# A staggered RWKV stage: the order of the chunks inside a step is reversed, and its stores are issued by ScalarE instead of GpSimd

## The chip, the cores and the metric

One Trainium2 chip, one of its cores. The metric is the device time of the whole program in microseconds (us), lower is better; a run gives one time, and the median of several is compared.

## The reference, cut to what matters

The program computes one inference step of two decoder layers. The change lies in layer 0 alone: the RWKV-7 scan over 2048 prompt tokens (8 heads of 64), and the S5 state-space layer (32 groups of 16 channels, 64 complex states each) that runs beside it.

```python
def rwkv7_scan(r, decay, k, v, aa, bb, s0):
    def step(s, inp):
        r_t, w_t, k_t, v_t, a_t, b_t = inp
        sa = jnp.einsum('bhvk,bhk->bhv', s, a_t)
        s = s * w_t[:, :, None, :] + sa[..., None] * b_t[:, :, None, :] + v_t[..., None] * k_t[:, :, None, :]
        return s, jnp.einsum('bhvk,bhk->bhv', s, r_t)
...
# s5_mixer: h = associative scan of abar * h + B u, per group
y = jnp.einsum('btgp,gcp->btgc', h_re, c_re) - jnp.einsum('btgp,gcp->btgc', h_im, c_im)
y = jax.nn.gelu(y.reshape(bsz, t, D_B) + d_skip * u)
```

## The kernel before, in words

The program is a row of stages with a barrier between any two: projections, the stage of this study (`rwkv_chunks`, names `rc_...`), the samples, an output stage, and the second layer. Everything is float32. In every stage each engine has its own list of instructions, and semaphores order them; an engine executes its list strictly in order.

`rwkv_chunks` cuts the 2048 tokens into 32 chunks of 64. One chunk goes through 16 phases, and in nearly all of them TensorE makes small 64x64 products (eight tiles, four of them side by side in the array), after which either ScalarE copies the PSUM banks to SBUF or VectorE masks or adds them, and the next phase of the same chunk needs that result:

- phase 0 (`M_`): products of the operands (L1652, L1655); VectorE masks them (L1800, L1802, L1806).
- phase 1 (`KV`): L1664, L1668; ScalarE copies all of it (L1766, 1,024 elements a partition). In phase 2 GpSimd masks a part in place (L1842).
- phases 2 to 11: five levels of a triangular inverse. The even ones (U0 to U4; L1729 to L1741) end in a copy by ScalarE (L1782), the odd ones (X0 to X4; L1750, for X4 L1752) in a predicated copy by VectorE (L1826).
- phase 12 (`SOLVE`, L1675, copied by ScalarE L1770), phase 13 (`LINK`, L1683, VectorE L1809 and L1812), phase 14 (`STATE`, L1695 to L1701, VectorE L1821), phase 15 (`OUT`, L1708 to L1714, ScalarE L1776 into `yb`).

The chunks are staggered: chunk c is in phase t - 6c at step t (`LAG` is 6, `FLIGHT` is 3), 202 steps in all. So six steps make one chunk's worth of work, and in each of these six there are two or three chunks on the way, six phases apart: {0, 6, 12}, {1, 7, 13}, {2, 8, 14}, {3, 9, 15}, {4, 10}, {5, 11}. `running(t)` gives them in the order in which every engine writes them into its list: in the kernel before the newest chunk (lowest phase) first.

A chunk's result `yb` goes to memory by two DMAs (even chunks) or four (odd chunks), issued by GpSimd at the end of its part of phase 15 (L1848, L1852). `yb` has two buffers; ScalarE waits for the store of the chunk two before.

The S5 layer rides along: after the chunks' phases of a step, each engine appends its S5 part. VectorE makes tables (L1383, L1435, L1439 and others) in every step up to 103 and again between the two halves. In steps 52 to 68 TensorE transposes two groups of a table (L1343 to L1345), ScalarE copies them (L1296) and GpSimd stores them (L1323); the next transposes wait for that copy (`tb_ev`). In steps 103 to 139 and 165 to 201 one group is treated every two steps: TensorE L1353 at odd steps and L1367 to L1369 at even ones, VectorE rotations and a scan, GELU on ScalarE at odd steps (L1303), and a store by GpSimd (L1328). The next group's L1367 to L1369 wait for that GELU (`y_ev`).

Of the kernel before, what the change touches and what calls it, by code (L numbers as in the profile page):

```python
# [25 lines left out]
SEQ = 2048  # L26
# [4 lines left out]
NCH = SEQ // CH  # L31
# [183 lines left out]
class Tail:  # L215
# [229 lines left out]
    def gpsimd(self, pool):  # L445
        def weights(k):
            pool.wait_ge(self.w_high, k + 1)
            low_part(pool, self.wl[:, k], self.wr[:, k % 4], self.wh[:, k]).then_inc(self.w_low[0], 1)

        def low(t):  # L450
            h, n = t % 2, self.rows(t)
            c = slice(h * P, h * P + n) if t < TT else slice(0, n)
            pool.wait_ge(self.c_high, t + 1)
            low_part(pool, self.cl[h][:, :, 0:n], self.cb[t // 2 % 2][:, :, c], self.ch[h][:, :, 0:n]).then_inc(self.c_low, 1)
        weights(0)
        weights(2)
        low(0)
        weights(4)
        weights(6)
        for t in range(1, TT + 1):  # L460
            low(t)
# [705 lines left out]
G, SP_, GC = 32, 64, 16  # L1167
T8 = 8
NC8 = SEQ // T8
HG = G // 2  # L1170
# [4 lines left out]
class StateSpace:  # L1175
# [102 lines left out]
    def scalar(self, act, t):  # L1278
        c_ = lambda n: self.sc[:, n, :]
        if t == self.BEGIN:  # L1280
            act.wait_ge(self.cst, 16 * self.MAPS)
            act.activation(c_(0), self.pt[:, 2, :], ACT.Exp).then_inc(self.act0, 1)
        if t == self.BEGIN + 2:
            act.wait_ge(self.angles, 1)
            act.activation(c_(1), c_(14), ACT.Exp)
            act.activation(c_(20), c_(14), ACT.Exp, scale=float(T8)).then_inc(self.act0, 1)
        if t == self.BEGIN + 4:
            act.wait_ge(self.angles, 2)
            act.activation(c_(5), c_(4), ACT.Sin)
            act.activation(c_(6), c_(4), ACT.Sin, scale=0.5).then_inc(self.act0, 1)  # L1290
        i = t - self.LT - 1
        if 0 <= i < HG:
            act.wait_ge(self.tb_pe, i + 1)
            if i >= 2:
                act.wait_ge(self.bi_st[i % 2], 16 * (i // 2))
            act.copy(self.bi[i % 2][:, :, :].rearrange("p a c -> p (a c)"), self.bx[:, :]).then_inc(self.tb_ev, 1)  # L1296
        g = self.group(t - 3)
        if g is not None:
            q = g % 2
            act.wait_ge(self.y_pe, g + 1)  # L1300
            if g >= 2:
                act.wait_ge(self.y_st[q], 16 * (g // 2))
            act.activation(self.yo[q][:, :], self.by[:, 0:NC8], ACT.Gelu_apprx_tanh).then_inc(self.y_ev, 1)  # L1303

    def scalar_end(self, act):
        for q in (0, 1):
            act.wait_ge(self.y_st[q], 16 * HG)
# [3 lines left out]
    def gpsimd(self, pool, t):  # L1311
        g = self.group(t + 1)
        if g is not None:
            k, at = g // 8, g % 8 * GC
            pool.wait_ge(self.tq_in[k % 2], 16 * T8 * (k // 2 + 1))
            if g >= 2:
                pool.wait_ge(self.y_pe, g - 1)
            pool.tensor_copy(self.tp[g % 2][:, :].rearrange("p (t c) -> p t c", t=T8),
                             self.tq[k % 2][:, :, at:at + GC]).then_inc(self.tp_ok, 1)
        i = t - self.LT - 1  # L1320
        if 0 <= i < HG:
            pool.wait_ge(self.tb_ev, i + 1)
            pool.dma_start(self.trans[:, i], self.bi[i % 2][:, :, :]).then_inc(self.bi_st[i % 2], 16)  # L1323
        g = self.group(t - 3)
        if g is not None:
            at = g % 8 * GC
            pool.wait_ge(self.y_ev, g + 1)
            pool.dma_start(self.y[at:at + GC, g // 8, 0:SEQ].rearrange("c (t n) -> t c n", t=T8), self.yo[g % 2][:, :]  # L1328
                           ).then_inc(self.y_st[g % 2], 16)

# [214 lines left out]
PHASES = 6 + 2 * LEVELS  # L1547
(M_, KV, U0) = range(3)
FLIGHT, LAG = 3, 6
SOLVE, LINK, STATE, OUT_ = range(PHASES - 4, PHASES)  # L1550
# [3 lines left out]
def rwkv_chunks(nc, ops, wc, const, y, s_out, space):  # L1554
# [7 lines left out]
    with Stage(nc, "rc") as s_:  # L1562
# [10 lines left out]
        yb = [s_.sb(f"yb{q}", [P, 4, CH]) for q in (0, 1)]  # L1573
# [16 lines left out]
        y_st = [s_.sem("y_st0"), s_.sem("y_st1")]  # L1590
        block = s_.block()
        half = [slice(0, 64), slice(64, 128)]
        quads = ((0, 0), (1, 1), (0, 1), (1, 0))
        tiles = [(g, r, s) for g in (0, 1) for r, s in quads]
        STEPS = LAG * (NCH - 1) + PHASES
        running = lambda t: [(c, t - LAG * c) for c in range(NCH - 1, -1, -1) if 0 <= t - LAG * c < PHASES]
        tokens = lambda c: slice(c * CH, (c + 1) * CH)
        every = lambda ap, n: ap.rearrange("p (o c) -> p o c", o=1).broadcast_to([P, n, ap.shape[-1]])
        flat = lambda ap: ap.rearrange("p s g c -> p s (g c)")
# [160 lines left out]
        @block.scalar  # L1760
        def _(act):
            def phase(c, ph):
                q, b = c % FLIGHT, bk[c % FLIGHT]
                if ph == KV:
                    act.wait_ge(k_pe, c + 1)
                    act.copy(kt[q][:, :, :, :].rearrange("p s k c -> p (s k c)"), b[:, :, :].rearrange("p s c -> p (s c)")  # L1766
                             ).then_inc(k_sb, 1)
                elif ph == SOLVE:
                    act.wait_ge(gh_pe, c + 1)
                    act.copy(hg[q][:, :, :, :, :].rearrange("p s g n c -> p s (g n c)"), b[:, :, 0:4 * CH]  # L1770
                             ).then_inc(gh_sb, 1)
                elif ph == OUT_:
                    act.wait_ge(y_pe, c + 1)
                    if c >= 2:
                        act.wait_ge(y_st[c % 2], STORES[c % 2] * (c // 2))
                    act.copy(yb[c % 2][:, :, :].rearrange("p (s k) c -> p s (k c)", s=2), b[:, :, 2 * CH:4 * CH]  # L1776
                             ).then_inc(y_sb, 1)
                elif U0 <= ph < SOLVE and ph % 2 == 0:
                    n = (ph - U0) // 2
                    act.wait_ge(u_pe[n], c + 1)  # L1780
                    lo, count = ((LV_u, 4), (LV_W, 3), (LV_u, 2))[min(n, 2)]
                    act.copy(lv[q][:, :, lo:lo + count].rearrange("p s k g c -> p s (k g c)"), b[:, :, 0:count * 2 * CH]  # L1782
                             ).then_inc(u_sb[n], 1)
            for t in range(STEPS):
                for c, ph in running(t):
                    phase(c, ph)
                s5.scalar(act, t)
            s5.scalar_end(act)
            for q in (0, 1):
                act.wait_ge(y_st[q], STORES[q] * NCH // 2)  # L1790
# [43 lines left out]
        @block.gpsimd  # L1834
        def _(pool):
            pool.wait_ge(cst, 64)

            def phase(c, ph):
                if ph == U0:
                    pool.wait_ge(k_sb, c + 1)  # L1840
                    k = kt[c % FLIGHT][:, :, 0:4].rearrange("p s k c -> p s (k c)")
                    pool.tensor_tensor(k, k, every(mask[:, :], 2), ALU.mult).then_inc(k_ok, 1)  # L1842
                elif ph == OUT_:
                    pool.wait_ge(y_sb, c + 1)
                    out = y[:, :, tokens(c)]
                    if c % 2 == 0:
                        for s in (0, 1):
                            pool.dma_start(out[:, s::2], yb[0][:, 2 * s:2 * s + 2, :]).then_inc(y_st[0], 16)  # L1848
                    else:
                        for r in (0, 1):  # L1850
                            for h in (0, 1):
                                pool.dma_start(out[half[h], r::2], yb[1][half[r], 2 * h:2 * h + 2, :]  # L1852
                                               ).then_inc(y_st[1], 16)
            for t in range(STEPS):
                for c, ph in running(t):
                    phase(c, ph)
                s5.gpsimd(pool, t)
# [1147 lines left out]
def program(nc, I, O):  # L3005

    def scratch(name, shape):
# [11 lines left out]
    space = (u, I["s5_par"], I["s5_mats"], I["s5_skip"], I, y_b, O["s5_p"], (kept_l, kept_m, kept_a),  # L3019
             scratch("s5_trans", (P, G // 2, 2, 2 * P)), scratch("s5_lags", (15 * GC, G * GC)))  # L3020
    rwkv_chunks(nc, ops, wc, I, y_a, O["rwkv_p"], space)
    even_samples(nc, vecs, I["state_rwkv"], O["rwkv_s"], y_a, u_s, I["s5_in"], kept_l, kept_m, kept_a, I["s5_drow"], I, y_b,
                 O["s5_s"])
# [129 lines left out]
```

## Time and profile before

| | us |
|---|---|
| median of 3 runs | 3392.26 |
| lowest, highest | 3385.58, 3393.54 |
| the profiled execution, its own time | 3385.58 |
| its span, first to last instruction | 3383.8 |
| the stage `rwkv_chunks` in it | 672 to about 1256 |
| TensorE, VectorE, ScalarE, GpSimd busy in the whole span | 2894.4, 2180.0, 1232.0, 823.6 |

The span is 1.8 us shorter than the time of the same execution. Times in the rows are microseconds from the span's start. PE is TensorE's matmul, PEld its weight load, DVE is VectorE, ACT ScalarE, POOL GpSimd, SP SyncE; a q behind an engine marks its sequencer, where DMAs are issued. One matmul in the source stands in the trace as two records or passes, since the operands are float32. Where a row says "issue", the engine waited for nothing that the profile shows.

### The profile page before, as it was taken

Reading aid. Unit: us, or ns where it says so; the run is one execution under the profiler, and the core shown is the slowest. Engines: PE = TensorE matmul, PEld = TensorE weight load, DVE = VectorE, ACT = ScalarE, POOL = GpSimd, SP = SyncE. Lnnn points to the kernel's source line nnn. Section 1 sums busy time; section 2 is a strip of 40 time slices with the busy share of each in tenths; the row PEclk is TensorE's granted clock in tenths of the full one; section 3 lists DMA queues with packets and bytes.
Section 4 is the critical chain, followed back from the end, with each engine's and each line's share of the span. In section 5 each row is a group of like instructions: output and inputs, shape, how many; then the busy total and the mean of one; then the engine's idle time right before and its main releaser. Section 6 shows DMA issues by size and latency. Waiting matters only on the chain. (4 is left out here: it accounts for less than half of the span.)

```text
span 3383.8 us, 77001 instructions
## 1 busy us (share of the span) xinstructions
PE 2894.4 (86%) x31187; PEld 2423.5 (72%) x31187; DVE 2180.0 (64%) x3314; ACT 1232.0 (36%) x2205; POOL 823.6 (24%) x726
## 2 busy tenths in 40 slices
PE   8799999867788772899789999997878898987698
PEld 7699999866677651688589878775755666667476
DVE  3435566567677655777618777723437898886587
ACT  1015555433333322344111110101107888884432
POOL 4100000012222220211112111103115676664221
PEclk9899999989999995999889999998998999999899
DMA  4425545443434335464448999964541101006542
GB/s 162 166 79 147 158 145 153 139 98 94 110 98 114 92 110 161 140 175 137 148 147 253 360 329 356 333 220 154 178 128 62 64 1 64 14 14 187 193 149 89
DMA packets 468650, 500.76 MB, mean 148 GB/s; under 512 B 199169, under 2 KB 362226, under 8 KB 463290
## 3 DMA queue, kind: packets, MB, share of 16 engines
q1 hardware_dynamic: 371162, 332.45, 32.9%
q10 hardware_dynamic: 88176, 146.58, 12.5%
q0 software_dynamic: 8960, 16.81, 1.8%
q8 instruction: 248, 4.06, 0.5%
q14 instruction: 104, 0.85, 0.1%
HBM read 357.52 MB, written 138.41 MB: 147 GB/s over the span
## 5 line engine op out<-in xcount | busy, mean ns | idle before, releaser
L2487 POOL TENSOR_TENSOR sp_att<-sp_beta,sp_left 128x512 f32<-128x512 f32 (+3 forms) x320 | 317.9, 1003 | 195.7 <-DVE sp_left L2443 184.0
L102 PE MATMUL po_acc<-po_x_high,po_w_low 128*128 128x412 f32 (+1 forms) x840 | 306.0, 364 | 33.9 <-POOL po_w_low L95 15.0
L102 PE MATMUL pe_acc<-pe_x_high,pe_w_low 128*128 128x412 f32 (+1 forms) x840 | 304.8, 363 | 22.8 <-DVE pe_x_low L95 14.1
L103 PE MATMUL po_acc<-po_x_low,po_w_high 128*128 128x412 f32 (+1 forms) x840 | 298.6, 355 | 0.0
L104 PE MATMUL po_acc<-po_x_high,po_w_high 128*128 128x412 f32 (+1 forms) x840 | 298.1, 355 | 0.0
L104 PE MATMUL pe_acc<-pe_x_high,pe_w_high 128*128 128x412 f32 (+1 forms) x840 | 295.8, 352 | 0.0
L103 PE MATMUL pe_acc<-pe_x_low,pe_w_high 128*128 128x412 f32 (+1 forms) x840 | 295.8, 352 | 0.0
L2443 DVE TENSOR_TENSOR_SCAN sp_left<-sp_z,sp_left,sp_zero 128x512 f32<-128x512 f32 x192 | 235.3, 1266 | 14.1 <-ACT sp_z L2387 12.1
L2174 DVE TENSOR_TENSOR po_work<-po_work,po_q 128x1024 f32<-128x1024 f32 x128 | 173.2, 1353 | 83.6 <-DMA po_work<-in_cache_k 78.1
L102 PEld LDWEIGHTS po_acc<-po_x_high,po_w_low 128*128 128x128 f32 x840 | 161.9, 193 | 82.2 <-ACT po_o L801 33.2
L2379 ACT ACTIVATE sp_beta<-sp_z,sp_bias 128x512 f32<-128x512 f32 (+3 forms) x320 | 183.5, 631 | 72.1 <-PE sp_z L2318 44.2
L1842 POOL TENSOR_TENSOR rc_kt<-rc_kt,rc_mask 128x512 f32<-128x512 f32 x32 | 40.7, 1273 | 681.9 <-ACT rc_kt L1766 681.7
L801 ACT COPY po_o<-po_acc 128x412 f32<-128x412 f32 (+1 forms) x105 | 52.5, 500 | 391.9 <-PE po_acc L104 375.4
L1782 ACT COPY rc_lv<-rc_bk 128x512 f32<-128x512 f32 (+2 forms) x160 | 109.8, 715 | 217.7 <-PE rc_bk L1741 217.4
L102 PEld LDWEIGHTS pe_acc<-pe_x_high,pe_w_low 128*128 128x128 f32 x840 | 159.8, 190 | 36.7 <-issue 24.6
L2387 ACT ACTIVATE sp_z<-sp_z,sp_bias_neg 128x512 f32<-128x512 f32 (+3 forms) x320 | 179.7, 614 | 0.0
L2333 PE MATMUL sp_t<-sp_id,sp_att 128*128 128x128 f32 x1088 | 154.7, 280 | 24.2 <-ACT sp_aT L2393 18.9
L2333 PEld LDWEIGHTS sp_t<-sp_id,sp_att 128*128 128x128 f32 x1088 | 117.4, 142 | 67.8 <-issue 64.9
L2348 PE MATMUL sp_ob<-sp_aT,sp_v 128*64 128x128 f32 x2176 | 155.2, 281 | 9.1 <-DVE sp_g L2457 9.1
L103 PEld LDWEIGHTS po_acc<-po_x_low,po_w_high 128*128 128x128 f32 x840 | 162.1, 193 | 0.9
L104 PEld LDWEIGHTS po_acc<-po_x_high,po_w_high 128*128 128x128 f32 x840 | 161.8, 193 | 0.7
L103 PEld LDWEIGHTS pe_acc<-pe_x_low,pe_w_high 128*128 128x128 f32 x840 | 159.6, 190 | 1.6
(453 smaller groups left out, 7308.3 us busy)
## 6 DMA issues: line engine op xcount, KB each, us to landing
po_work<-in_cache_k SPq DMA_DIRECT2D x256, 256.0 KB, 4.9
po_work<-in_cache_v ACTq DMA_DIRECT2D x256, 256.0 KB, 4.5
scratch_ops<-pe_work SPq DMA_DIRECT2D x160, 128.0 KB, 2.0
out_z<-pe_o SPq DMA_DIRECT2D x84, 206.0 KB
out_z<-po_o ACTq DMA_DIRECT2D x84, 206.0 KB
pe_w<-in_w_e SPq DMA_DIRECT2D x21, 512.0 KB
po_w<-in_w_o ACTq DMA_DIRECT2D x21, 512.0 KB
rc_opx<-scratch_ops SPq DMA_DIRECT2D x16, 640.0 KB, 6.1
```

The lines of the kernel that those rows point to most:

```text
L102: pe.matmul(out, ll, rh, start=start, stop=False)
L103: pe.matmul(out, lh, rl, start=False, stop=False)
L104: return pe.matmul(out, lh, rh, start=False, stop=stop)
L801: copy(self.ot[:, t % self.PIECES, 0:hi - lo], bank[:, 0:hi - lo]).then_inc(self.evicted, 1)
L1782: act.copy(lv[q][:, :, lo:lo + count].rearrange("p s k g c -> p s (k g c)"), b[:, :, 0:count * 2 * CH]).then_inc(u_sb[n], 1)
L2174: dve.tensor_tensor(kp[:, p % KR], kp[:, p % KR], qb[:, b % 2:b % 2 + 1, :].broadcast_to([P, 2, CW]), ALU.mult).then_inc(prod, 1)
L2333: mm = pe.transpose(tb[h][:, b * P:(b + 1) * P], att[h][:, n % 3, b * P:(b + 1) * P], idt[:, :])
L2348: mm = pe.matmul(ob[tile(n) % 2][c, 0:P], vt[m % 2][:, 4 * g + b, c], aT[h][:, n % 2, b * P:(b + 1) * P], start=(diagonal(n) and b == 0), ...
L2379: act.activation(be[h][:, n % 4, 0:w], zb[h][n % 2][:, 0:w], ACT.Sigmoid, scale=DC ** -0.5, bias=bt[:, head:head + 1]).then_inc(sig[h], 1)
L2387: act.activation(zb[h][n % 2][:, 0:w], zb[h][n % 2][:, 0:w], ACT.Sigmoid, scale=-DC ** -0.5, bias=nbt[:, head:head + 1]).then_inc(kept[h], 1)
L2443: dve.tensor_tensor_scan(row[:, at:at + w][:, ::-1], zb[h][n % 2][:, 0:w][:, ::-1], zero.broadcast_to([P, w]), start, ALU.mult, ALU.add).t ...
L2487: pool.tensor_tensor(att[h][:, n % 3, 0:w], be[h][:, n % 4, 0:w], left[h][tile(n) % 2][:, at + 1:at + 1 + w], ALU.mult).then_inc(at_ok[h], 1)
```

## The change

Two things change, both in the stage `rwkv_chunks`.

1. `running(t)` lists the chunks of a step in ascending order: the oldest chunk (highest phase) comes first, the newest last. All four engines' lists are reordered alike. No instruction is added or taken away by this.
2. All stores of the stage are issued by ScalarE. Right behind the copy (or GELU) that fills the buffer it waits for its own semaphore and issues the DMAs: two or four per chunk (`yb`), one per S5 group (`yo`), one per step of the transposes (`bi`). GpSimd keeps the masking and the copies of `tq`.

```diff
@@ StateSpace.scalar
             act.copy(self.bi[i % 2][:, :, :].rearrange("p a c -> p (a c)"), self.bx[:, :]).then_inc(self.tb_ev, 1)
+            act.wait_ge(self.tb_ev, i + 1)
+            act.dma_start(self.trans[:, i], self.bi[i % 2][:, :, :]).then_inc(self.bi_st[i % 2], 16)
...
             act.activation(self.yo[q][:, :], self.by[:, 0:NC8], ACT.Gelu_apprx_tanh).then_inc(self.y_ev, 1)
+            act.wait_ge(self.y_ev, g + 1)
+            act.dma_start(self.y[at:at + GC, g // 8, 0:SEQ].rearrange("c (t n) -> t c n", t=T8), self.yo[q][:, :]
+                          ).then_inc(self.y_st[q], 16)
@@ StateSpace.gpsimd
-        i = t - self.LT - 1
-        if 0 <= i < HG:
-            pool.wait_ge(self.tb_ev, i + 1)
-            pool.dma_start(self.trans[:, i], self.bi[i % 2][:, :, :]).then_inc(self.bi_st[i % 2], 16)
...
-            pool.wait_ge(self.y_ev, g + 1)
-            pool.dma_start(self.y[at:at + GC, g // 8, 0:SEQ].rearrange("c (t n) -> t c n", t=T8), self.yo[g % 2][:, :]
-                           ).then_inc(self.y_st[g % 2], 16)
@@ rwkv_chunks
-        running = lambda t: [(c, t - LAG * c) for c in range(NCH - 1, -1, -1) if 0 <= t - LAG * c < PHASES]
+        running = lambda t: [(c, t - LAG * c) for c in range(NCH) if 0 <= t - LAG * c < PHASES]
@@ rwkv_chunks, scalar, phase OUT_ (and taken out of gpsimd, phase OUT_)
+                    act.wait_ge(y_sb, c + 1)
+                    out = y[:, :, tokens(c)]
+                    if c % 2 == 0:
+                        for s in (0, 1):
+                            act.dma_start(out[:, s::2], yb[0][:, 2 * s:2 * s + 2, :]).then_inc(y_st[0], 16)
+                    else:
+                        for r in (0, 1):
+                            for h in (0, 1):
+                                act.dma_start(out[half[h], r::2], yb[1][half[r], 2 * h:2 * h + 2, :]
+                                              ).then_inc(y_st[1], 16)
```

## Rows read from the trace of the kernel before

**Rows 1.** Page, part 1: busy time, share of the span, instructions.
```profile
PE 2894.4 (86%) x31187; PEld 2423.5 (72%) x31187; DVE 2180.0 (64%) x3314; ACT 1232.0 (36%) x2205; POOL 823.6 (24%) x726
```

**Rows 2.** Stage by stretches: start:end, length, busy (count), clock, DMA share, GB/s.
```profile
708.40:824.80 116.40, 81.27 (x3604) 73.56 (x3604) 88.95 (x171) 38.24 (x59) 22.37 (x28) 0.96 0.35 76
824.80:869.00 44.20, 33.86 (x1144) 31.65 (x1144) 25.53 (x56) 16.58 (x30) 12.94 (x20) 1.00 0.42 122
869.00:948.20 79.20, 57.64 (x2580) 51.48 (x2580) 58.09 (x158) 27.73 (x44) 17.97 (x24) 0.98 0.40 97
964.30:1073.20 108.90, 102.94 (x3232) 84.92 (x3232) 76.91 (x195) 38.13 (x66) 33.47 (x55) 1.00 0.49 119
1073.20:1158.30 85.10, 58.37 (x2569) 52.20 (x2570) 57.66 (x125) 26.87 (x42) 16.87 (x23) 0.96 0.34 77
```

**Rows 3.** Waits of PE, 676 to 1245 us: total us, times, longest.
```profile
PE rc_bk L1738 <- issue: 19.9, 16, 3.4
PE rc_bk L1664 <- DVE rc_m L1802: 17.7, 17, 5.6
PE rc_s_x L1343 <- ACT rc_s_bi L1296: 11.8, 12, 1.4
```

**Rows 4.** DMA queues, 676 to 1245 us: packets, MB, share of 16 engines.
```profile
q8 instruction: 132, 2.16, 1.6%
```

**Rows 5.** Stretches between two pauses of PE (columns as in rows 2).
```profile
721.09:726.10 5.01, 3.15 (x128) 2.79 (x131) 3.74 (x9) 1.66 (x3) 0.00 (x0) 1.00 0.06 16
...
762.15:766.03 3.88, 2.52 (x128) 2.17 (x127) 2.93 (x6) 1.50 (x2) 0.00 (x0) 1.00 0.17 35
```

**Rows 6.** Timeline of PE, one such stretch: start, us, instruction, [idle before <- releaser].
```profile
762.15 0.39 PE L1738 MATMUL rc_bk<-rc_xx,rc_m 64*64 64x64 f32 x10 [0.74 <-issue]
762.32 0.45 PE L1741 MATMUL rc_bk<-rc_id,rc_xx 64*64 64x64 f32 x16
762.55 0.45 PE L1738 MATMUL rc_bk<-rc_xx,rc_m 64*64 64x64 f32 x16
...
766.03 0.38 PE L1750 MATMUL rc_bk<-rc_lv 64*64 64x64 f32 x9 [1.34 <-issue]
```

**Rows 7.** Timelines of ACT, then PE, then DVE, over phases 5 and 0.
```profile
784.49 0.80 ACT L1782 COPY rc_lv<-rc_bk 128x768 f32<-128x768 f32 x1 [0.33 <-PE rc_bk L1741]
786.69 0.58 ACT L1782 COPY rc_lv<-rc_bk 128x512 f32<-128x512 f32 x1 [1.40 <-PE rc_bk L1741]
...
787.33 0.62 PE L1752 MATMUL rc_bk<-rc_lv 64*64 64x64 f32 x14 [0.45 <-ACT rc_lv L1782]
...
791.01 0.72 PE L1664 MATMUL rc_bk<-rc_opx 64*64 64x128 f32 x13 [1.42 <-DVE rc_m L1802]
...
788.06 0.45 DVE L1826 COPY_PREDICATED rc_lv<-rc_lev,rc_bk 128x256 f32<-128x256 int32 x1 [0.69 <-PE rc_bk L1752]
788.40 0.68 DVE L1383 TENSOR_TENSOR rc_s_tmp<-rc_s_m,rc_s_sc 128x512 f32<-128x512 f32 x1
...
789.84 0.42 DVE L1800 TENSOR_TENSOR rc_xx<-rc_bk,rc_lev 128x256 f32<-128x256 f32 x1
790.18 0.68 DVE L1802 TENSOR_TENSOR rc_m<-rc_bk,rc_mask 128x512 f32<-128x512 f32 x1
```

**Rows 8.** Timeline in the stretch of the transposes.
```profile
841.64 0.33 PE L1343 MATMUL rc_s_x<-rc_s_id,rc_s_cos 128*128 128x128 f32 x1 [1.43 <-ACT rc_s_bi L1296]
...
843.18 0.59 ACT L1296 COPY rc_s_bi<-rc_s_x 128x512 f32<-128x512 f32 x1 [1.59 <-DMA scratch_s_trans<-rc_s_bi]
```

**Rows 9.** DMA issues: one on ACT's timeline; a line of SP, ns min/median/max.
```profile
41.50 0.33 ACTq L210 DMA_DIRECT2D scratch_u<-pu_o  x1
...
L1614 SPq DMA_DIRECT2D rc_opx<-scratch_ops x64: 586/646/1508, 680.9 to 1195.0; - x64
```

**Rows 10.** Groups of the whole span: busy us, mean ns | idle before.
```profile
L1303 ACT ACTIVATE rc_s_yo<-rc_s_y 128x256 f32<-128x256 f32 x32 | 12.4, 387 | 9.6 <-PE rc_s_y L1369 9.6
...
L1353 PE MATMUL rc_s_x<-rc_s_xT,rc_s_bi 128*128 128x256 f32 x128 | 36.2, 405 | 0.0
```

More of the change, by code:

```diff
@@ L1296, in scalar @@
             act.copy(self.bi[i % 2][:, :, :].rearrange("p a c -> p (a c)"), self.bx[:, :]).then_inc(self.tb_ev, 1)
+            act.wait_ge(self.tb_ev, i + 1)
+            act.dma_start(self.trans[:, i], self.bi[i % 2][:, :, :]).then_inc(self.bi_st[i % 2], 16)
         g = self.group(t - 3)
         if g is not None:
-            q = g % 2
+            q, at = g % 2, g % 8 * GC
             act.wait_ge(self.y_pe, g + 1)
@@ L1319, in gpsimd @@
                              self.tq[k % 2][:, :, at:at + GC]).then_inc(self.tp_ok, 1)
-        i = t - self.LT - 1
-        if 0 <= i < HG:
-            pool.wait_ge(self.tb_ev, i + 1)
-            pool.dma_start(self.trans[:, i], self.bi[i % 2][:, :, :]).then_inc(self.bi_st[i % 2], 16)
-        g = self.group(t - 3)
-        if g is not None:
-            at = g % 8 * GC
-            pool.wait_ge(self.y_ev, g + 1)
-            pool.dma_start(self.y[at:at + GC, g // 8, 0:SEQ].rearrange("c (t n) -> t c n", t=T8), self.yo[g % 2][:, :]
-                           ).then_inc(self.y_st[g % 2], 16)
     def tensor(self, pe, t):
@@ L1842, in phase @@
                     pool.tensor_tensor(k, k, every(mask[:, :], 2), ALU.mult).then_inc(k_ok, 1)
[L1843 to L1853, printed above, removed]
             for t in range(STEPS):
```

## The prediction

> **What bounds the kernel now.** I read the page first, then the stage by stretches, then PE's waits in it, the DMA queues, and timelines. TensorE is busy 86% of the span [rows 1], and the change touches one stage of some 580 us. There the stretches differ [rows 2]. In two of them, where S5 groups run, PE is at its work: from 964 to 1073 it is busy 102.94 of 108.90, and from 1158 to 1245 it is alike. The rest is different: in 708 to 825 PE is busy 81.27 of 116.40, though ACT is busy only 38.24 and DVE 88.95. So there something paces PE that is not an engine's work.
>
> The waits say what. The largest is "issue" [rows 3], and on the timeline such pauses cut PE's list in regular pieces: one at 762.15, the next at 766.03, in the middle of a row of equal matmuls, with 128 matmuls and 127 or 128 weight loads between them [rows 5, 6]. The instruction queue moved 132 transfers of 2.16 MB in 569 us [rows 4]: 16 KB each, which is 64 bytes for each of 256 instructions. So PE eats one such block and waits for the next. A block that ends in a pause takes 3.88 us [rows 5]; I read others of 3.3 to 3.9, and take 3.7 as the pace of this supply. The work in a block is far less: sixteen small matmuls start every 0.23 us (762.32, 762.55) [rows 6], 128 take about 2 us. A chunk is 512 matmuls, exactly four blocks: at least 4 x 3.7 = 14.8 us. Measured: 116.40 / 7 = 16.6 us [rows 2]. Three of the four blocks run at the supply's pace, the fourth takes 5.01 [rows 5]: it is the one over phases 4, 5 and 0, and is bound by dependences. (The Trainium skill, "Runtime: NRT & Kernel Launch", Instruction fetch mechanics, has the 16 KB blocks of 256 instructions too, but calls their cost mostly hidden; the trace disagrees, with pauses of 0.74 and 1.34 us. What its rule would make of the time is the third rival.)
>
> **The reordering.** It adds no instruction; it decides which waits fall outside the supply's pause. In the slow block [rows 7] PE waits 0.45 for the copy of U4 (ACT 786.69, 0.58 long, begun only when the pause was over, since U4 came last), then runs X4, M, U2, SOLVE, and waits 1.42 for the mask of M: DVE does X4's copy at 788.06, two table operations from 788.40, and reaches M's product at 789.84, M's mask at 790.18; PE goes on at 791.01. New order, same cut (7 matmuls before the end of phase 4's work, which is now U1's): U4 was finished before the pause and its copy too, so X4 starts at once (0.1 to 0.56). U1's copy (0.80 long [rows 7]) starts 0.3 after the pause: X1 at 1.15 to 1.4. Its masked copy by DVE ends at 2.05, U2 2.15 to 2.6 (SOLVE, 0.46, fits before it), M to 3.3, then the first quarter of LINK to 3.55. The wait for M's mask moves to KV, behind LINK and X2 (1.15 us of cover against 1.4 us of DVE: 0.3 is left, in a block with 1.3 of slack). So this block falls from 5.0 to about 3.8. Elsewhere the order loses cover (U0 to X0, X0 to U1, X3 to U4: 0.3 to 0.6 each), but in blocks of 2.0 to 2.5 us of work, under the 3.7. DVE has 88.95 / 7 = 12.7 us of work a chunk [rows 2] in a cycle of 15.3, still enough.
> - 708 to 825: 7 chunks x -1.2 = -8.
> - 1073 to 1158: the same cut within ten matmuls, 17.0 a chunk: 5 x -1.2 = -6.
> - 869 to 948: after the transposes the cut lies elsewhere and no block is as slow, 79.20 / 5 = 15.8 a chunk [rows 2]: 5 x -0.6 = -3.
>
> Bounds: all 17 chunks to 14.8 gives -28; if DVE's tables or lost cover push one block a chunk 0.5 over the pace, -8.
>
> In the S5 stretches PE is at its work (108.90 / 6 = 18.1 us a chunk), and L1353 (36.2 / 32 = 1.13 us a group [rows 10]) or L1367 to L1369, which take longer, lie behind each step's phases as cover: 0 for the order alone.
>
> **The transposes (824.8 to 869).** Here PE waits in each step for ACT's copy (0.98 to 1.43 us [rows 3, 8]), which stands in ACT's list behind the copies of the step's phases. With KV last in its step (its copy takes 1.0) the wait grows by 1.15, with U0 last by 0.65, and with SOLVE first it shrinks by 0.7: over 16 steps about +2.5. Blocks take over 5 us here, so no pause hides it.
>
> **The stores on ScalarE.** ACT spends no time on a store except its issue: 0.33 us where each partition holds one run [rows 9], and for stores in runs of 256 bytes to strided rows I take SP's issues of the same shape, 0.65 (least 0.59, worst 1.5) [rows 9]. Bounds: 0.33 and 1.5. A chunk costs ACT 1.2 (even) or 2.6 us (odd), an S5 store 0.6, a transposed table 0.4. What is queued behind:
> - Without S5: behind OUT's copy come U4's and U1's copies. OUT's matmuls end 0.35 into a block of 3.7, ACT is through at 0.35 + 0.2 + 0.37 + 2.6 = 3.5, and U4's copy is wanted only behind the pause. Odd chunks lose 0.1 to 0.3, even ones nothing: +2.
> - With transposes: the table's copy waits behind OUT's four stores (+2.2 at step 57) and two (+0.9 at step 63): +3. ACT no longer waits for a slot that GpSimd's queue released late (1.59 [rows 8]): -1.5.
> - With S5 groups: after OUT, PE has X3 and X0 (0.46), L1353 (1.13), U4 and U1 (1.15), in all 2.75 us before L1367, which waits for the GELU (0.387 [rows 10]). ACT needs 0.2 + 0.37 + 2.6 + 0.39 + 0.1 = 3.7 on odd chunks: +1.0 for each of the four (17, 19, 27, 29), nothing on even ones (2.3): +4.
> - GpSimd loses its issues, and nobody waits for it: 0.
>
> (The Trainium skill, "DMA: Bandwidth & Descriptors", Issuing engines are not separate DMA queues, speaks against the move: all issuers share the same 16 DMA engines, and who issues saves only sequencer time. The trace shows that time at 0.33 and 0.65; by it the move alone can only cost, as here.)
>
> **The sum.** -17 + 2.5 + 2 + 3 - 1.5 + 4 = -7 us. The profiled execution took 3385.6 and would take 3378.6; it was the fastest of three, and the median is 3392.3, so I forecast 3385.
>
> **The rivals.**
> 1. *The forecast*, -7, own range -20 to +5. Chance 0.50.
> 2. *Slower: ScalarE becomes late.* Place: phase 15 of odd chunks. SP issues 8 to 12 loads of its own at 0.65 in the same steps, and its single issues reach 1.5 [rows 9]. If two queues issuing together make it 1.0 each, four take 4.0, and the copies of U4 and U1 begin 1.3 later: 16 x 1.3 = 21, transposes +2, S5 +1.3 x 4 = +5 on top of -7: about +20, 3412. It decides from 0.7 us an issue on. For: no slack beyond 0.3 in my count of the odd chunks. Against: SP's median is the same over the whole stage. Chance 0.23.
> 3. *No supply pace: dependences alone.* If the pauses of "issue" were no supply of instructions, a cycle is PE's own 8.8 us (512 matmuls at 0.23 for sixteen, LINK, X4 and a few others at half the width) plus waits of 0.45, 1.42 and some 0.3, 11.0 in the old order, and 10.9 in the new one, where the waits are other ones but sum to the same, so the order gives nothing, and the stores lie on it in full (+1.2 to +1.7 on odd chunks, +0.5 on even ones): +25 with the rest. The pauses at 128 matmuls speak against it. It would look like rival 2. Chance 0.03. This is where the skill's "mostly hidden" would lead.
> 4. *The supply alone sets the pace*: the slow block is slow by a clock drop or by late blocks and stays so. The order brings 0 to -5, the stores +5: 3392. Chance 0.12.
> 5. *Faster*: ScalarE's issues at 0.35 cost nothing, and the order brings its full -20: 3370. Chance 0.12.
>
> **How the numbers follow.** 0.3% is 10 us, about what a measurement of this kernel can tell from no change. Faster by more: case 1's lower part (0.21) and case 5 (0.12) = 0.33. Within: 0.28 of case 1, 0.12 of case 4, 0.02 of case 2 = 0.42. Slower: 0.01 of case 1, 0.21 of case 2, 0.03 of case 3 = 0.25. The range reaches from near case 5 to between 1 and 2: 3366 to 3407. As large signs oppose each other, the likeliest case's own range is 3372 to 3397.
>
> **What would show it.** In the new profile: (a) in 708 to 825 the chunks take 15.3 to 15.5 us, the waits of L1664 for L1802 (17.7) nearly vanish, and "issue" grows, since blocks that waited for data now wait for instructions. (b) "L1343 <- ACT L1296" rises from 11.8 to 15 to 18. (c) ACTq shows 0.6 to 0.65 for the y_a stores; if it is 1.0 or more, case 2. (d) In S5 stretches new waits of L1367 for L1303, about 1 us, one every 36 us. (e) A q0 queue without this stage's packets. The forecast is wrong if the new order makes another block a chunk longer than 4.3 us (a cover that I undercounted, most likely X0 or KV behind DVE's tables), or if PE's clock, which fell to half for a few stretches of the stage (0.96 in its first [rows 2]), falls more often with more pauses: each fall costs up to 1.5 us.

## The result and the profile after

The change made the kernel slower: 3421.2 us (median of 6 runs, 3409.2 to 3426.5) against 3392.9 us (6 runs, 3385.6 to 3402.9), ratio 1.0083, 95% interval 1.0063 to 1.0101, or +28 us. I had forecast 3385 and a range up to 3407; the sign and the range were both missed. The profiled execution took 3415.2 us, its span is 3413.3. The traced execution of before is the fastest of its six (3385.6, median 3392.9), and that of after lies 6 us below its median too. A difference between two single traces can so be some 7 us off, and more where the other trace lies above its own median. Verdicts below go by the ratios, and places by the traces.

Page of the kernel after, part 1 (engine, busy us, share of the span, instructions), against [rows 1]:

```profile
PE 2914.7 (85%) x31187; PEld 2442.0 (72%) x31187; DVE 2163.1 (63%) x3314; ACT 1236.3 (36%) x2205; POOL 734.5 (22%) x582
```

GpSimd lost 144 instructions and 89 us of work, and nobody was waiting for it. The time was lost elsewhere: the stage is 22.9 us longer in the trace, and the other 6.6 us of the span lie scattered in later stages that the change doesn't touch.

Stretches of the stage, after (columns as in [rows 2]):

```profile
714.50:821.20 106.70, 76.18 (x3320) 68.57 (x3310) 83.78 (x153) 35.41 (x52) 8.18 (x7) 0.92 0.35 74
821.20:895.80 74.60, 53.55 (x1659) 50.60 (x1659) 32.37 (x89) 24.05 (x39) 3.96 (x3) 0.89 0.35 98
843.40:850.20 6.80, 4.44 (x90) 4.22 (x90) 1.15 (x2) 1.35 (x3) 0.00 (x0) 0.51 0.23 63
```

The granted clock is 0.92 where it was 0.96 in the first stretch, and 0.89 where it was 1.00 in the transposes. The third row is one of three pieces at half clock (the 1.2 GHz level; 0.51 in this window) inside the second: 822.8 to 826.2, 843.2 to 850.0 and 874.0 to 880.8, together 17 us. Before has none there. Cut at the same points of the work, the stretch of the transposes reads, first in before, then in after:

```profile
807.50:885.01 77.51, 59.44 (x2208) 54.98 (x2207) 49.42 (x120) 29.19 (x48) 21.50 (x32) 1.00 0.45 119
806.69:901.29 94.60, 67.08 (x2220) 63.09 (x2216) 46.23 (x120) 30.08 (x49) 5.24 (x4) 0.88 0.39 98
```

It is 17.1 us longer. PE is idle for 9.5 us more of it, and busy for 7.6 us more with the same work, at a clock of 0.88 for 1.00. So the loss there has two parts of nearly the same size, waits and clock.

PE's waits in the stage, after, 676 to 1290 us (total us, times, longest), against [rows 3]:

```profile
PE rc_s_x L1338 <- ACT rc_s_bi L1296: 19.8, 12, 4.2
PE rc_bk L1733 <- issue: 17.5, 19, 2.2
PE rc_bk L1690 <- DVE rc_rpt L1817: 15.5, 17, 1.1
...
PE rc_bk L1659 <- DVE rc_m L1807: 8.4, 13, 5.7
...
PE rc_s_y L1362 <- ACT rc_s_yo L1305: 4.1, 5, 1.4
```

L1338 here is L1343 of before, L1659 is L1664, L1362 is L1367. The wait for M's mask was halved, as meant (17.7 to 8.4), and a new one of nearly the old one's size stands beside it: STATE waits for the sum that VectorE makes of LINK's product (15.5). The wait for the transposed table's copy rose from 11.8 to 19.8, and its longest from 1.4 to 4.2.

The place of that 4.2, timeline of after in the transposes:

```profile
840.87 0.37 ACT L1771 COPY rc_yb<-rc_bk 128x256 f32<-128x256 f32 x1 [2.17 <-PE rc_bk L1709]
...
841.27 3.21 ACTq L1781 DMA_DIRECT2D scratch_y_a<-rc_yb  x4
...
844.88 0.59 ACT L1296 COPY rc_s_bi<-rc_s_x 128x512 f32<-128x512 f32 x1 [3.64 <-issue]
...
845.51 0.47 PE L1338 MATMUL rc_s_x<-rc_s_id,rc_s_cos 128*128 128x128 f32 x1 [4.25 <-ACT rc_s_bi L1296]
```

Read from the bottom: PE stood 4.25 us for the copy at 844.88; ScalarE could not begin it for 3.64 us, because for 3.21 of them it was issuing the four stores of an odd chunk; and PE's matmul behind the wait takes 0.47 where it took 0.33 [rows 8], since the clock fell to half at 843.2, inside the wait.

The stores' issues in after (ns min/median/max):

```profile
L1781 ACTq DMA_DIRECT2D scratch_y_a<-rc_yb x64: 529/627/1734, 735.2 to 1275.7; - x64
...
L1298 ACTq DMA_DIRECT2D scratch_s_trans<-rc_s_bi x16: 326/326/377, 823.5 to 894.1; - x16
```

The single price was forecast well (0.65 and 0.33). The four together take 2.93 us in the mean (2.51 to 3.67 over the 16 odd chunks), not 2.6.

### The profile page after: what moved, and what is told of

Same layout as the page of the kernel before. It is cut to its first block and busy times, and to the rows that moved or that the text cites. A ratio compares the mean times of both kernels' runs of the same rounds, so it can differ in the third digit from the quotient of the medians.

```text
span 3413.3 us, 77001 instructions
## 1 busy us (share of the span) xinstructions
PE 2914.7 (85%) x31187; PEld 2442.0 (72%) x31187; DVE 2163.1 (63%) x3314; ACT 1236.3 (36%) x2205; POOL 734.5 (22%) x582
## 5 line engine op out<-in xcount | busy, mean ns | idle before, releaser
L102 PE MATMUL po_acc<-po_x_high,po_w_low 128*128 128x412 f32 (+1 forms) x840 | 306.5, 365 | 34.6 <-POOL po_w_low L95 15.5
```

The costliest lines, as they stand in the source:

```text
L102: pe.matmul(out, ll, rh, start=start, stop=False)
```

## The experiments

Thirteen kernels ran. This table gives, for each, the ratio to before, and, from its trace, how much longer than before each stretch of the stage is, cut at the starts of ScalarE's SOLVE copies of chunks 0, 6, 10, 15, 21 and 26 and at the stage's end. In before the stretches are 99.1, 77.5 (with the transposes), 79.2, 109.0 (S5 groups), 85.0 and 99.6 us (S5 groups, and the end, up to the next stage's first instruction at 1257.87).

```
kernel                        ratio  [95% interval]     0-6   6-10  10-15  15-21  21-26  26-end
after                         1.0083 [1.0063, 1.0101]  -1.7  +17.1  +1.5   +3.1   -2.4   +4.4
e1_order_only                 1.0009 [0.9996, 1.0022]  -2.8   +6.9  +4.2   +4.8   -2.5   +4.8
e2_stores_only                1.0082 [1.0059, 1.0106]  +3.7  +11.3  +1.9   +7.2   -1.7   +6.0
e3_newest_first_52_68         1.0064 [1.0040, 1.0089]  +2.1  +16.1  +0.5   +4.8   -5.0   +5.1
e4_table_copy_first           1.0006 [0.9991, 1.0021]  +1.0   -4.2  +3.6   +4.4   -1.9   +6.7
e5_chunk_stores_only          1.0080 [1.0062, 1.0098]  +4.0  +14.0  +0.3   +5.6   +2.6   +2.3
e6_s5_stores_only             1.0015 [1.0002, 1.0028]  +0.6   +1.7  +2.1   +1.2   -2.7   -1.1
e7_before_table_first         0.9990 [0.9977, 1.0003]  +0.1   -5.4  +0.7   -1.2   -0.7   -2.2
e8_light_loads                0.9947 [0.9929, 0.9964]  -1.0   +0.4  -1.6   -1.5   -4.0   -2.2
e9_light_loads_reordered      0.9945 [0.9928, 0.9962] -10.5   +5.5  -2.6   +1.3   -9.1   +0.4
e10_stores_last_in_step       1.0040 [1.0027, 1.0053]  -0.1  +10.5  +0.8   +4.3   -4.5   +4.6
e11_spare_copies              1.0040 [1.0027, 1.0053]  +0.7   +9.8  +5.6   +0.8   -2.4   +1.3
e12_stores_last_table_first   1.0009 [0.9999, 1.0020]  -0.1   -5.4  +2.9   +2.7   -2.2   +3.7
e13_light_loads_after         1.0012 [1.0002, 1.0023]  -5.1  +18.7  -2.1   +2.9   -5.6   +4.0
```

Kernels with the same lists in a stretch show how far its time can be trusted: after, e3 and e4 differ by up to 3.8 us in the first stretch and by up to 3.1 in the fifth, and e2 and e3, which are alike in steps 52 to 68, by 4.8 in the second. So a difference of less than 4 or 5 us in one stretch of one trace shows nothing by itself. And the traced execution of e1 took 3408.4, 7.4 above its kernel's median, that of e4 7.9 and that of e8 6.5 above, while before's lies 7.3 below, so their stretches sum to more than the ratio says (e1: +15.4 for +3); those of e6, e7, e11 and e12 lie 9 to 14 below.

**The two parts apart.** e1 is before with one line changed; e2 is after with that line put back.

```diff
-        running = lambda t: [(c, t - LAG * c) for c in range(NCH - 1, -1, -1) if 0 <= t - LAG * c < PHASES]
+        running = lambda t: [(c, t - LAG * c) for c in range(NCH) if 0 <= t - LAG * c < PHASES]
```

> Only the order of the chunks in a step is reversed (oldest first); all stores stay with GpSimd. The changed kernel lost 22.9 us in this stage, about 16 of them in steps 52 to 68 (the transposes). Theory A (the order lengthens the transposes' wait, the stores on ScalarE lengthen it again, and the order gains nothing elsewhere): stage +10 to +14 us against before, with +8 to +10 of it in the transposes. Theory B (the stores on the hardware queue collide with SP's loads and hold up PE's instruction supply; the order is harmless): stage -5 to +3. Theory C (the order alone costs it all): +20 or more.

> Only the stores move to ScalarE; the order stays newest first. Theory A: stage +8 to +12 us, nearly all in the transposes and on odd chunks beside S5 groups. Theory B: +18 to +25, spread over the whole stage, with longer pauses of PE at every 128th matmul. Theory C: 0 to +4.

The order alone is worth +3 us (-1 to +7), the stores alone +28: the stores carry the loss, and the order brings none of the gain. Of the recorded theories none came true for e2: A had +8 to +12, and B, nearer in size with +18 to +25, wanted longer pauses at every 128th matmul, where PE's waits of "issue" sum to 62 us for 74 in before. For e1, A had the place (the transposes, +6.9 for 8 to 10), not the size by the ratio. Waits of PE in e2, 676 to 1290 us:

```profile
PE rc_s_x L1338 <- ACT rc_s_bi L1296: 16.3, 12, 4.5
PE rc_bk L1745 <- ACT rc_lv L1787: 15.8, 15, 3.1
...
PE rc_s_y L1362 <- ACT rc_s_yo L1305: 8.6, 6, 2.3
```

The first is 11.8 in before [rows 3], the GELU's is not in before's list at all, and the second reads there:

```profile
PE rc_bk L1750 <- ACT rc_lv L1782: 5.3, 9, 1.1
```

Three waits for ScalarE grew: table +4.5, U's copies +7.7, GELU +8.6. (For U's copies the line shown grew by 10.5; the other one that waits for them, L1747, L1752 of before, fell from 4.1 to 1.3.) They don't say by themselves where the time went. In the three stretches without S5's groups and without transposes e2 is only 3.9 us longer (3.7 + 1.9 - 1.7) and e5 below, with OUT's stores alone, 6.9; in the transposes they are 11.3 and 14.0 longer, and in the two with S5's groups together 13.2 and 7.9. An odd chunk without S5, ScalarE and then PE in e2:

```profile
801.04 0.37 ACT L1771 COPY rc_yb<-rc_bk 128x256 f32<-128x256 f32 x1 [2.87 <-PE rc_bk L1709]
801.45 2.50 ACTq L1781 DMA_DIRECT2D scratch_y_a<-rc_yb  x4
803.99 1.29 ACT L1787 COPY rc_lv<-rc_bk 128x768 f32<-128x768 f32 x2 [2.57 <-issue]
...
804.84 0.70 PE L1745 MATMUL rc_bk<-rc_lv 64*64 64x64 f32 x16 [0.95 <-ACT rc_lv L1787]
```

Even where the four issues take their least, 2.50, the copies of U4 and U1 start only then, and PE waits 0.95. In the three stretches like this one such waits grew by 4.0 us together, about what e2 loses there.

**The transposes: order or list?** e3 is after with the old order in steps 52 to 68 only; e4 is after with the table's copy and its store taken to the front of ScalarE's step.

```diff
@@ e3
-        running = lambda t: [(c, t - LAG * c) for c in range(NCH) if 0 <= t - LAG * c < PHASES]
+        running = lambda t: [(c, t - LAG * c) for c in (range(NCH - 1, -1, -1) if 52 <= t <= 68 else range(NCH))
+                              if 0 <= t - LAG * c < PHASES]
@@ e4, the lines of "i = t - self.LT - 1" and the "if" below it moved out of StateSpace.scalar into scalar_first
             for t in range(STEPS):
+                s5.scalar_first(act, t)
                 for c, ph in running(t):
```

> The changed kernel, but in steps 52 to 68 the newest chunk comes first as before; stores on ScalarE throughout. Theory A: 8 to 10 us faster than the changed kernel, the stretch of the transposes near that of the stores-only kernel. Theory B: no more than 2 us faster. Theory C: the whole +16 of the stretch goes.

> The changed kernel with one more edit: in steps 53 to 68 ScalarE makes the copy (and store) of the transposed table at the start of its step, ahead of the chunks' copies, so that the transposes no longer wait behind them and behind OUT's stores. Theory A (the wait of L1338 for the copy is what the stretch lost): the wait of PE for that copy (19.8 us in the trace, more where it is hidden) nearly vanishes, the stretch falls by 20 us or more, and the kernel is back at the time of before or a little under it. Theory B: the stretch falls as well, but by less than 10, since the supply of instructions sets its pace.

e3 gave back 6 us by the ratio, which its interval and after's can't tell from nothing, and its transposes are no shorter in the trace (+16.1 for +17.1); Theory A had 8 to 10. e4 gave back 26 us of 28, as its Theory A said, and its transposes are 4.2 us shorter than those of before (21.3 shorter than after's, with PE's wait for the table's copy down from 19.8 to 1.2). What stands ahead of the table's copy in ScalarE's list decides, with all 144 issues still on ScalarE.

**Which stores, and is the list a gain for before too?** e5 is before with the change's two hunks of phase OUT_ alone (OUT's stores on ScalarE), e6 is before with its two hunks in StateSpace.scalar and StateSpace.gpsimd alone (the table's and S5's stores); e7 is before with the edit of e4, its store left with GpSimd:

```diff
+                s5.scalar_first(act, t)
                 for c, ph in running(t):
                     phase(c, ph)
                 s5.scalar(act, t)
```

> Before, with the stores of OUT's result alone moved to ScalarE; S5's stores stay with GpSimd, the order is the old one. All stores on ScalarE cost 27 us. Theory A (OUT's two or four stores, 2.2 to 3.2 us in a row, stand ahead of the transposed table's copy and of the GELU): nearly all of it comes back, 3415 to 3422, ratio 1.0055 to 1.0075, the transposes 9 to 12 us longer. Rival B (two queues, SP's and ScalarE's, each slow the other's issues, so every store that ScalarE issues costs alike): by the share of issues, 80 of the 144 are OUT's, about +15, 3408. Rival C (the S5 stores do it, which are the last in ScalarE's step): +3 or less.

> Before, with the stores of the transposed table and of S5's result alone moved to ScalarE. Theory A: 0.33 us an issue for the table and 0.62 for S5's result, both at the end of ScalarE's step with nothing queued that is wanted at once, and the table's copy no longer waits for a slot: 0 to +3 us, ratio 0.9995 to 1.001. Rival B: +12, ratio 1.0035. Rival C: +20 or more, ratio 1.006.

> Before, with the transposed table's copy put first in ScalarE's list of its step, ahead of the phases' copies; stores stay with GpSimd, order as before. Theory A (PE's wait for this copy in each of the 16 steps is time on the path, 11.8 us by the waits): faster by 8 to 16 us, 3377 to 3385, ratio 0.9955 to 0.9975; the transposes shrink by 8 to 12. Rival D (what the copy gains, the phases' copies lose, since they are wanted in the same step): within 3 us of before.

Theory A held in kind for e5 and e6, each a little over its range (+27 us, the transposes +14.0 for 9 to 12; and +5 for 0 to +3). e7 fell short: -3.6 us (-8 to +1), though 5.4 us in the transposes. Its waits there:

```profile
PE rc_bk L1740 <- issue: 4.7, 4, 2.9
PE rc_s_x L1345 <- ACT rc_s_bi L1284: 3.1, 1, 3.1
```

The wait for the table fell from 11.8 to 3.1, and some of what it freed turned into waits for instructions (4.7, where before has 2.6 at that line): 8.7 us of wait were worth 5.4 us of time in that stretch. That the kernel as a whole gains is not shown. Against e7, e4 differs by the change itself, order and stores, and costs 5 us more (1.0006 - 0.9990; -2 to +12 by the two intervals): with the table's copy in front, the whole change is worth +5, not +28.

**Is it the hold, or the transfer?** (Hold: the time for which ScalarE's list stands still.) e10 issues OUT's stores at the very end of ScalarE's step, behind the table's copy and the GELU. e11 is before, all stores with GpSimd, and holds ScalarE with needless copies behind OUT's copy:

```diff
@@ e10, the stores taken out of phase OUT_ into stores(c)
                 s5.scalar(act, t)
+                for c, ph in running(t):
+                    if ph == OUT_:
+                        stores(c)
@@ e11, in phase OUT_
+                    for n in range((2, 4)[c % 2]):
+                        act.copy(spare[:, 512 * n + 512:512 * n + 1024], spare[:, 0:512]).then_inc(spared, 1)
```

> The whole change, with OUT's two or four stores moved from behind OUT's copy to the very end of ScalarE's step, behind the transposed table's copy and the GELU. Still 144 issues on ScalarE, the same bytes in the same queue. Theory A (what counts is what stands behind the stores in ScalarE's list): nearly all of the 28 us comes back, 3395 to 3402, ratio 1.0005 to 1.0025; the wait of PE for the table's copy falls from 19.8 to 12 or 13, with none above 2 us. Rival B (the issues and transfers of the stores themselves, by contention with SP's issues and the instruction blocks): 3415 or more, ratio 1.0065 or more.

> Before, its stores with GpSimd as they were, with two (even chunks) or four (odd ones) needless ScalarE copies of 512 columns, some 0.6 us each, behind OUT's copy: ScalarE is held for as long as by the stores, but issues none. Theory A: as slow as with the stores there, 3412 to 3422, ratio 1.005 to 1.0085, and the transposes 8 to 12 us longer. Rival B: within 5 us of before, ratio under 1.0015. In between (1.002 to 1.005): both have a part.

Both came out in the middle, at half the loss (+14 us each), which by the words recorded for e11 would mean that hold and issues both have a part. In e10 the wait for the table's copy fell from 19.8 to 14.9 only, its longest from 4.2 to 3.2, where I had 12 or 13 and none above 2. For e11:

```profile
838.97 2.18 ACT L1782 COPY rc_spare<-rc_spare 128x512 f32<-128x512 f32 x4
...
841.05 0.58 ACT L1296 COPY rc_s_bi<-rc_s_x 128x512 f32<-128x512 f32 x1
...
841.68 0.47 PE L1343 MATMUL rc_s_x<-rc_s_id,rc_s_cos 128*128 128x128 f32 x1 [3.05 <-ACT rc_s_bi L1296]
```

Needless copies do the same harm at the same place, half clock behind it included, but four of them hold ScalarE 2.18 us. The stores of e5 held it 3.00 at this chunk and PE waited 4.20; over the stage they hold it 2.8 (odd) and 1.3 us (even), the copies 2.2 and, by halves, 1.1. That is 16 x 0.6 + 16 x 0.2 = 13 us less, an estimate, and the two kernels differ by 14, so the shorter hold can be the reason for the smaller loss. It is not shown to be: e11's copies hold ScalarE for 53 us in all and cost 14, the stores of e5 for 66 us and cost 27, so only the last 13 us would have cost a microsecond each. What e11 shows is that a hold without any store does half of the harm, at the same place. Against a large part of the issues or transfers themselves speaks e4, where all of them are still on ScalarE and only their place in the list is another.

e10 shows that within the transposes the end of the step is no free place either:

```profile
843.09 3.51 ACTq L1766 DMA_DIRECT2D scratch_y_a<-rc_yb  x4
...
846.64 1.29 ACT L1788 COPY rc_lv<-rc_bk 128x512 f32<-128x512 f32 x2 [3.94 <-issue]
847.81 0.60 ACT L1296 COPY rc_s_bi<-rc_s_x 128x512 f32<-128x512 f32 x1
...
848.47 0.47 PE L1338 MATMUL rc_s_x<-rc_s_id,rc_s_cos 128*128 128x128 f32 x1 [3.21 <-ACT rc_s_bi L1296]
```

Behind the table's copy of its own step, the stores are ahead of the U copies and the table's copy of the next.

e12 has the edits of e4 and e10 together.

> The whole change with both repairs: the transposed table's copy first in ScalarE's step, OUT's stores last. It is the best version of the change that I can make from the runs. Table first alone took 24 us off the change and 3.6 off the kernel before. If the two repairs mend the same wait: 3393 to 3398, ratio 1.000 to 1.0015. If the stores last also mend the stretches beside S5's groups (12 us there): 3384 to 3390, ratio 0.9975 to 0.999.

It is the best version of the change that I ran: +3 us (0 to +7), its transposes 5.4 us shorter than those of before. It joins e4's gain there; the first of the two recorded ranges held. Beside S5's groups it saves nothing that can be told (+2.7 and +3.7 for +3.1 and +4.4 in after), although PE's waits for the GELU, 4.1 us in after, are gone in e10 and e12: those waits are not what after loses there. No version beats before by more than can be measured.

**Does the load of the queues matter?** e8 is before, e9 e1, and e13 after, each with SP's loads of the chunks' operands cut to 16 of 128 partitions from chunk 4 on: as many issues, an eighth of the bytes, and an output of other data.

```diff
-                        sp.dma_start(dst[half[r], 2 * h:2 * h + 2], src[half[h], 2 * r:2 * r + 2]).then_inc(sem, 16)
+                        sp.dma_start(dst[64 * r:64 * r + m, 2 * h:2 * h + 2], src[64 * h:64 * h + m, 2 * r:2 * r + 2]
+                                     ).then_inc(sem, 16)
...
-                                           ops[:, :, :, tokens(c)], ops_in[c % 2])
+                                           ops[:, :, :, tokens(c)], ops_in[c % 2], 8 if c >= 4 else 64)
```

> Before, with SP's loads of the chunks' operands moving 16 of 128 partitions from chunk 4 on (same number of issues, an eighth of the bytes; the output is then other data's). It asks whether the pauses between blocks of 128 matmuls are instruction blocks that come late behind the data loads. Theory E (they are late because of the loads): the pauses of 1.3 to 2.5 us shrink to 0.7 or less, the stretches at half clock behind them vanish, a chunk takes 14.8 to 15.5 instead of 16.6, and the stage is 20 to 35 us shorter: 3360 to 3377. Rival F (a block's fetch takes its 3.3 to 3.9 whatever else moves): the pauses stay within 0.3, the stage within 5 us.

> The same light loads with the phases in the new order (oldest chunk first), stores on GpSimd. If my prediction's step on the order failed only because late blocks and half clock covered its gain (theory E), it shows here: 8 to 17 us below the light loads alone. If the order has no gain of its own (the waits only change their names: STATE for LINK's table instead of KV for M's mask), it is within 4 us of the light loads alone, or up to 4 slower by the transposes.

> The whole change with the light loads (16 of 128 partitions of the chunks' operands from chunk 4 on; other data's output). With the light loads the kernel before took 0.9947 of before, the new order 0.9945. Theory A: the stores on ScalarE cost their 8 to 12 us in the transposes and some beside S5 whatever SP loads: 3392 to 3400, ratio 1.000 to 1.0025. Rival B (the store issues are slow because SP's loads burst in the same time): 3376 to 3384, ratio 0.995 to 0.9975, ScalarE's longest issue under 0.8 us instead of 1.7.

For the stores it doesn't: with light loads they cost 1.0012 - 0.9945, 23 us, with full ones 1.0083 - 1.0009, 25 us. Rival B fell, and e13's Theory A held. For the order the kernel's time shows nothing, with full loads (+3) or with light ones (0.9947 and 0.9945): of what I had recorded for e9, the second case came. In the stretch ahead of the transposes it does matter. One chunk in e1, cut into its four blocks:

```profile
748.20:752.02 3.82, 2.35 (x141) 2.08 (x133) 3.45 (x5) 1.60 (x2) 1.31 (x1) 1.00 0.50 113
752.02:756.71 4.69, 2.32 (x131) 2.08 (x132) 3.33 (x6) 0.96 (x2) 1.42 (x2) 1.00 0.65 139
756.71:761.60 4.89, 4.43 (x128) 4.19 (x129) 2.16 (x4) 1.97 (x3) 0.00 (x0) 0.65 0.01 3
761.60:765.70 4.10, 2.90 (x137) 2.65 (x136) 4.00 (x9) 1.01 (x1) 0.58 (x1) 1.00 0.01 4
```

in e9:

```profile
750.60:754.30 3.70, 3.12 (x129) 2.74 (x128) 2.87 (x6) 1.97 (x3) 0.00 (x0) 1.00 0.02 4
754.30:758.40 4.10, 2.89 (x134) 2.65 (x134) 3.98 (x9) 1.01 (x1) 0.56 (x1) 1.00 0.02 4
758.40:761.40 3.00, 2.33 (x146) 2.06 (x134) 2.93 (x5) 1.60 (x2) 0.71 (x1) 1.00 0.08 17
761.40:765.00 3.60, 2.40 (x131) 2.13 (x132) 3.24 (x6) 0.96 (x2) 2.27 (x4) 1.00 0.21 45
```

and in e8, the old order:

```profile
752.50:757.45 4.95, 3.04 (x127) 2.68 (x126) 3.54 (x8) 1.66 (x3) 0.00 (x0) 1.00 0.02 6
757.45:761.30 3.85, 2.90 (x134) 2.63 (x128) 3.34 (x6) 1.01 (x1) 1.27 (x1) 1.00 0.02 5
761.30:764.60 3.30, 2.52 (x128) 2.17 (x127) 2.25 (x5) 1.50 (x2) 0.00 (x0) 1.00 0.12 27
764.60:768.20 3.60, 2.09 (x127) 1.96 (x128) 3.50 (x7) 1.17 (x2) 1.71 (x4) 1.00 0.11 25
```

In these rows the new order takes a chunk with light loads from 15.7 to 14.4 us; over the six chunks of the stretch, from 16.4 to 14.8. The slow block is gone (4.95, now 3.70 and 4.10). With full loads the same order has a block of 4.69 under a DMA share of 0.65 (it ends in a pause of 1.99), and the next one, 128 matmuls at a clock of 0.65, takes 4.89. Before has such late blocks too:

```profile
778.20:782.60 4.40, 2.56 (x130) 2.21 (x129) 3.36 (x6) 1.50 (x2) 0.00 (x0) 1.00 0.74 169
```

Over chunks 0 to 6 the order is worth -9.5 us with light loads (e9 against e8). With full ones it is -2.8 (e1 against before) or -5.4 (after against e2). Theory E is half right. The kernel's time fell as it said (3373, ratio 0.9947), and the clock rose (without the drop at the stage's end, before has 24 us at half clock in it and e8 7). But in the old order the light loads change the first stretch by only -1.0, to 16.4 us a chunk where E had 14.8 to 15.5, so there the pauses are not the loads' doing. Against e8, e9 then loses 5.1 us in the transposes and 2.8 and 2.6 in the stretches with S5's groups, and gains 5.1 in 21 to 26; 5 us are left in the traces, and by the ratios the two are equal. Of the 18 us of e8 its trace shows 10 in the stage; as it lies above its kernel's median and before's below, the traces can't settle the rest.

## Why the prediction was wrong

The sum was -7 us and the kernel took +28. Two terms failed by nearly as much each: the order with its transposes (-14.5, measured +3) and the stores (+7.5, measured +25 to +28). With either of them right the time would have come out inside my range, by 1 to 4 us: 3392.9 + 3 + 7.5 or 3392.9 - 14.5 + 25 to 28. The stores failed at the slack that I gave ScalarE in the transposes and beside S5's groups, and at the half clock that went with PE's waits there, which no term had; the order failed at a gain of 1.2 us a chunk that was mostly not kept. Point by point, by its own steps:

- **Supply blocks.** Right: the pauses every 128 matmuls are there in every kernel. What I took for a constant, 3.7, is not one: the two blocks shown with a DMA share of 0.65 and 0.74 take 4.69 and 4.40. (The Trainium skill, "Runtime: NRT & Kernel Launch", Instruction fetch mechanics, calls this cost mostly hidden; after shows waits of "issue" up to 2.2 us at one line. The trace disagrees here as before.)
- **The order, -17, and the same with the transposes, -14.5.** Measured +3. The step that failed is the gain at a constant pace of supply, -1.2 for each of twelve chunks and -0.6 for five. In 708 to 825 (-8) it brought -2.8 to -5.4; with light loads it brought -9.5, so the count of dependences was good there, and part of the gain seems to go where the block that gains time is followed by one that comes late anyway, as in the rows of e1 (4.69, a pause of 1.99, then 4.89 at a clock of 0.65). In 869 to 948 (-3) and 1073 to 1158 (-6) it brought +4.2 and -2.5 by e1, -0.4 and -0.7 by after against e2: next to nothing. In the transposes I had +2.5, and it is +6.9, +5.8 (after against e2) and +5.1 with light loads; PE's wait for the table's copy grew by only 0.8 in e1, but the clock there is 0.92 for 1.00. (I also had blocks "over 5 us" there and no pause; they take 4.9, 44.20 us for 1,144 matmuls [rows 2], and from 807.5 to 885 PE has 5.0 us of "issue".) Beside the S5 groups, where I put 0, e1 has +4.8 in each stretch and after against e2 -4.1 and -1.6: whether the order costs anything there stays open, and so does why light loads don't turn the gain of the first stretch into time of the kernel.
- **The stores, +2 +3 -1.5 +4 = +7.5.** Measured +25 to +28. Each price was right (0.63 and 0.33 an issue; four take 2.9 for 2.6). The term that was missed most is the transposes: 3 - 1.5 forecast, 11.3 (e2) to 14.0 (e5) measured. I had +2.2 for a table's copy behind four stores; it was 3.3 (1.0 to 4.25). And I gave the wait no aftermath, where the clock of that stretch fell to 0.90 in e2 and 0.88 in after: in the piece shown PE's 4.44 us of work would be about 2.2 at full speed, an estimate, and there are three pieces, of 3.4, 6.8 and 6.8 us. Next come the S5 groups: 4 forecast, 7.9 to 13.2 measured, of which the waits for the GELU explain part at most. The term without S5, +2, measured 3.9 to 6.9: I let U4's copy be "wanted only behind the pause", for 0.1 to 0.3 us an odd chunk; it is 0.95 in the chunk shown.
- **GpSimd's late slot, -1.5.** The table's issue on ScalarE does land in time (in after ScalarE has no wait for a store of the table), and the gain can't be told from the rest.
- **The rivals.** Rival 2 named the place (ScalarE late on odd chunks) and the sign, with +20. Its price, 1.0 us an issue because two queues issue together, did not come: the 96 issues of OUT's stores take 0.71 in the mean, the 59 that overlap an issue of SP 0.71 and the 37 others 0.72, and light loads change nothing. Most of its sum was 16 x 1.3 for the copies of U4 and U1, where PE's waits grew by 7.7, and it had only 2 more than I in the transposes, where the stores cost 11 to 14; that its +20 is near +28 is in part luck. Rival 4's reading of the order (0 to -5) was near, its +5 for the stores was not. Rival 3 gave +25 for a wrong reason: the pauses are real.
- **The signs to look for.** (a) failed: a chunk takes 16.2 where I wrote 15.3 to 15.5 (97.4 us for six), the wait of L1664 was halved but not gone, and "issue" did not grow: over all lines it fell from 74 to 53 us. (b) was low: 19.8 for 15 to 18. (c) held. (d) held in kind: L1362, 4.1 us in five waits. (e) held: in this stage q0 has no packets. The last one came true as well: the clock fell more often. Without the long drop that begins a few microseconds before its end, the stage runs at half clock for 24 us in before, 55 in after, 58 in e1 and 75 in e2.

On the move itself this case agrees with the Trainium skill, "DMA: Bandwidth & Descriptors", Issuing engines are not separate DMA queues, by which another issuer saves only the time of the issue. Here that time was saved on GpSimd, which nobody waited for, and spent on ScalarE, at 0.63 us an issue, and nothing came back for it: +25 to +28 us.

## What to carry to other kernels

Before a DMA issue is moved to another engine, write down what stands behind it in that engine's list, for every kind of step, and count issue time x number as a hold on those; an engine that is busy 36% of the time can still have no gap at that place. Weigh the hold by place: where PE had pauses of its own, holds of 2.5 to 3.7 us on every odd chunk cost 4 to 7 us in all, but where PE waited for ScalarE in every step, they cost 11 to 14 us in 77; in after about half of that stretch's loss came through the clock. And put what the slowest engine waits for at the front of the helper's step before anything else: that one move took 26 us off the change.

## What the hardware showed that I had not expected

- Long waits of PE were often paid twice: with the one of 4.25 us came 6.8 us at half clock, behind 1.99 us a block at 0.65, and in e11 behind a wait of 3.05, made with nothing but ScalarE copies, matmuls of 0.47 in place of 0.33. It is not so each time: in e6 PE waited 3.17 us up to 751.76, and its clock from 746 to 760 is 1.00.
- The pace of instruction blocks goes with what else the DMA engines move. In the stretches of before without S5's groups, of the blocks between two pauses at full clock, the 14 with a DMA share of 0.65 or more take 4.4 us in the mean (3.6 to 5.6), the 24 with less than 0.5 take 3.8 (3.35 to 4.9).
- A ScalarE issue of a store takes 0.33 us in whole rows and 0.63 in 256-byte pieces, and up to 1.73; that spread stays with light loads (longest 1.5), so SP's bytes are not its cause.
